# A one-core transformer layer with routed experts: activations turned by VectorE in 32x32 squares, expert weights loaded in consecutive rows

## The chip, the cores and the metric

The kernel runs on one core of one Trainium2 chip. The metric is device time in microseconds: 712.67 as the median of three runs (710.99 to 712.89). PE is TensorE (PEld its weight loads), DVE is VectorE, ACT is ScalarE, POOL is GpSimd, and SP is the queue that issues the large loads. All data are float32.

## The reference

One layer over 512 latent tokens and 256 context tokens, width 1024: modulated norm, one input projection, neighbourhood attention beside a bidirectional recurrence, an output projection with a gated residual, and then a mixture of 16 experts of which each token takes two. The part around the change is the last:

```python
def _moe(h, router_w, router_b, w1, w3, w2):
    aff = jax.nn.sigmoid(jnp.einsum('bld,de->ble', h, router_w))
    ...  # the best group of 4 experts, the top 2 experts in it, gates that add up to one
    for e in range(N_EXPERTS):
        y = (jax.nn.silu(h @ w1[e]) * (h @ w3[e])) @ w2[e]
        out = out + gates[..., e:e + 1] * y
```

w1 and w3 are 1024 x 512 for each expert, w2 is 512 x 1024; h is the normed latent stream, scaled and shifted by two rows computed from the condition vector. All weights of all experts are read once: 16 times 6.3 MB.

## The kernel before

**The expert loop.** The router sorts the (token, expert) pairs into tiles of 32 rows, each tile of one expert; in these data there are 44. PE keeps 32 rows as its loaded operand and lets 256 columns of weights pass, with four column groups of the array working on four quarters of the outputs. So a row of 1024 numbers lies as four quarters of 256 on four groups of 32 partitions, and a tile is a square of 128 partitions x 256.

For tile n the work is this. POOL fetches the rows by index from DRAM (`gather`, L478, buffer `xg`, two of them). ACT copies them (`next_rows`, L730, into `xrow`), PE turns the copy in two 128x128 pieces (`turn_rows`, L1606), DVE scales (L1238) and shifts (L1240) the result into `hsT`. PE multiplies by w1 and w3 (`products`, L1598: 8 slices of 128 inputs, 4 column groups). ACT takes the Silu of one half (L719) and DVE multiplies by the other (L1244) into `eact`. PE turns `eact` (`turn_act`, L1611), ACT copies it to `eT` (L723). PE multiplies by w2 (`rows_out`, L1621), DVE applies the gate (L1251), and POOL adds the rows by index into a DRAM array (`scatter`, L482). Before each fetch and each store by index, ACT copies a column of indices (L736, L742).

**The order around it.** It is written out by hand for each engine, and each engine goes strictly in its order. PE's is: products(n), turn_rows(n+1), rows_out(n-1), turn_act(n). ACT's is: Silu(n), copy of the turned activations(n), copy of the rows n+2, index for the fetch of n+4, index for the store of n-1. POOL's is the store of tile n-1, then the fetch of tile n+4. A buffer `xg` is fetched again once it was copied, so each fetch hangs on the copy of the tile two before it.

**The weights.** SP loads them in chunks of 2 MB, three to an expert: two of w1 and w3 together (L308, 128 partitions x 4 pieces of 2 KB for each matrix) and one of w2 (L311, 128 partitions x 4 pieces of 4 KB). There are 11 places for chunks (`homes`); chunk n takes the place of chunk n-11 after the last tile that used it (`sp.wait_ge(yt_ps if part == 2 else h_ps, after)`). The stores and fetches by index go over another queue of the same 16 DMA engines.

**Earlier users of the same layout.** The scale and shift rows `ab2` are summed over partitions by PE (`reduce_mod`, L1366, four times) and biased by DVE (`reduced`, L910). `router` (L1541) turns the normed tokens for the routing product, 32 turns in all.

## Time and profile before

| | us |
|---|---|
| median of 3 runs | 712.67 |
| lowest and highest | 710.99, 712.89 |
| the profiled execution | 713.67 |
| its span | 711.9 |
| expert loop, first product to the last `rows_out` | 423.36 to 697.15 |

The page gives 634.1 us (89%) of PE busy, 339.1 of DVE, 232.0 of ACT and 176.3 of POOL. Busy sums say little here: matmuls overlap, and each stage has another limit. The chain of waits tells which engine's work the end hung on; the windows tell how full the DMA engines were (their share can pass 1 because packets overlap) and how much they moved.

### The profile page before, as it was taken

What the parts mean: (1) busy time and instruction counts of PE and PEld (TensorE: products, weight loads), DVE (VectorE), ACT (ScalarE), POOL (GpSimd) and SP (SyncE); (2) the same over time, 40 slices, a digit from 0 to 9 for tenths busy, and PEclk for the clock granted to TensorE, in tenths of its full rate; (3) what the DMA queues carried; (4) which work ended last, traced back from release to release, by engine and by line L of the source; (5) the groups of instructions that cost most, each with busy time, mean ns of one, the idle gap of its engine ahead of it and who ended that gap; (6) DMA issues with size and microseconds to landing.
All of it is one profiled execution on the core that took longest, in us unless ns stands there. A gap on an engine that the chain in (4) does not pass through costs nothing.

```text
span 711.9 us, 15114 instructions
## 1 busy us (share of the span) xinstructions
PE 634.1 (89%) x5905; PEld 348.9 (49%) x5905; DVE 339.1 (48%) x794; ACT 232.0 (33%) x600; POOL 176.3 (25%) x201
## 2 busy tenths in 40 slices
PE   0799999899998997999999349999999999999991
PEld 0446544445444444555557325555555555555550
DVE  4513999456777957777662622222222222222220
ACT  5312201258887114555457101221122212222110
POOL 3033781000000001000003022344444444344431
PEclk9999999989999999999998559999999999999996
DMA  7999438711205359400048992999999999999924
GB/s 220 387 313 290 131 118 292 239 60 36 81 1 177 115 188 267 124 2 1 1 180 293 408 361 81 370 382 380 378 377 379 378 382 375 379 383 384 331 35 133
DMA packets 83508, 167.55 MB, mean 235 GB/s; under 512 B 4149, under 2 KB 26321, under 8 KB 83457
## 3 DMA queue, kind: packets, MB, share of 16 engines
q1 hardware_dynamic: 71856, 145.78, 56.6%
q0 software_dynamic: 11472, 21.00, 11.8%
q8 instruction: 38, 0.62, 0.4%
q14 instruction: 14, 0.11, 0.0%
q10 hardware_dynamic: 128, 0.04, 0.0%
HBM read 155.52 MB, written 12.60 MB: 236 GB/s over the span
## 4 chain that ended last, share of the span: by engine, by line
PE 66%; DVE 17%; issue 6%; DMA 4%; ACT 4%; SPq 1%; POOLq 0%; DVEq 0%
PE bank L1598 23%; PE bank L1621 12%; PE bank L1516 7%; PE bank L1408 7%; DMA ring<-in_w_mod_dram 4%; PE bank L1333 3%; DVE acct L880 3%; DVE gax L880 3%; PE bank L1606 2%; PE bank L1493 2%; PE bank L1479 2%; PE bank L1468 2%; DVE pre L898 2%; PE bank L1611 2%; PE bank L1297 1%
## 5 line engine op out<-in xcount | busy, mean ns | idle before, releaser
L1408 PE MATMUL bank<-ring,hx 128*128 128x512 f32 x256 | 115.0, 605 | 2.7 <-DVE mix L933 2.7
L482 POOL DMA_INDIRECT out_quarters<-pre,cur_s x44 | 69.6, 1582 | 146.9 <-ACT cur_s L742 124.4
L1244 DVE TENSOR_TENSOR pre<-pre,bank 128x128 f32<-128x128 f32 x44 | 12.7, 288 | 161.9 <-ACT pre L719 147.2
L1408 PEld LDWEIGHTS bank<-ring,hx 128*128 128x128 f32 x256 | 49.0, 194 | 60.2 <-issue 59.5
L1598 PE MATMUL bank<-pre 128*32 128x256 f32 x1248 | 75.0, 386 | 2.1 <-DVE pre L1240 1.4
L1598 PE MATMUL bank<-ring,pre 128*32 128x256 f32 x1152 | 67.6, 380 | 0.2
L1516 PE MATMUL bank<-ring,mix 128*128 128x512 f32 x128 | 61.8, 604 | 0.2 <-DVE mix L1038 0.2
L1598 PEld LDWEIGHTS bank<-pre 128*32 128x32 f32 x1248 | 41.7, 111 | 26.8 <-issue 3.0
L719 ACT ACTIVATE pre<-bank 128x128 f32<-128x128 f32 x44 | 12.2, 278 | 118.6 <-PE bank L1598 118.6
L1598 PEld LDWEIGHTS bank<-ring,pre 128*32 128x32 f32 x1152 | 37.7, 110 | 22.4 <-issue 1.4
L1333 PE MATMUL bank<-hx,ring 128*128 128x256 f32 (+1 forms) x128 | 43.7, 502 | 1.4 <-DVE hx L858 1.4
L723 ACT ACTIVATE pre<-bank 128x128 f32<-128x128 f32 x44 | 12.2, 278 | 96.5 <-PE bank L1611 96.5
L1621 PE MATMUL bank<-pre 128*32 128x256 f32 x704 | 42.5, 382 | 0.6 <-DVE pre L1251 0.6
L1251 DVE SCALAR_TENSOR_TENSOR pre<-bank,hx,pre 128x256 f32<-128x256 f32 x44 | 21.3, 484 | 43.9 <-PE bank L1621 43.9
L451 POOL DMA_DIRECT2D pre<-pre x1 | 0.6, 563 | 154.9 <-ACT pre L656 154.9
L1333 PEld LDWEIGHTS bank<-hx,ring 128*128 128x128 f32 x128 | 24.7, 195 | 20.2 <-issue 17.6
L1621 PE MATMUL bank<-ring,pre 128*32 128x256 f32 x544 | 32.9, 382 | 0.0
L461 POOL DMA_DIRECT2D xn_quarters<-pre x4 | 2.2, 545 | 115.9 <-DVE pre L1057 115.6
L880 DVE SCALAR_TENSOR_TENSOR acct<-ring,cs,acct 128x256 f32<-128x256 f32 x56 | 29.1, 520 | 2.0
L1516 PEld LDWEIGHTS bank<-ring,mix 128*128 128x128 f32 x128 | 22.0, 193 | 15.2 <-issue 14.8
L1621 PEld LDWEIGHTS bank<-pre 128*32 128x32 f32 x704 | 20.8, 109 | 15.5 <-issue 3.5
L1340 PE MATMUL bank<-hx,ring 128*128 128x512 f32 x64 | 27.6, 592 | 0.0
(282 smaller groups left out, 1019.5 us busy)
## 6 DMA issues: line engine op xcount, KB each, us to landing
pre<-in_exp_w_dram SPq DMA_DIRECT2D x28, 1024.0 KB
ring<-in_exp_w_dram SPq DMA_DIRECT2D x24, 1024.0 KB
ring<-in_w_mod_dram SPq DMA_DIRECT2D x16, 1024.0 KB, 5.1
pre<-in_exp_w_dram SPq DMA_DIRECT2D x8, 2048.0 KB
ring<-in_exp_w_dram SPq DMA_DIRECT2D x6, 2048.0 KB
ring<-in_w_in_dram SPq DMA_DIRECT2D x5, 2048.0 KB, 16.8
ring<-in_w_mod_dram SPq DMA_DIRECT2D x4, 2048.0 KB, 19.4
mix<-in_exp_w_dram SPq DMA_DIRECT2D x6, 1024.0 KB
```

Of the source, the lines that this page charges most:

```text
L482: g.indirect_dma_start(out=acc_dram, out_offset=bass.IndirectOffsetOnAxis(ap=cur_s[par][:].bitcast(U32), axis=0), in_=ysb[par], in_offset= ...
L880: ins = v.scalar_tensor_tensor(out=dst, in0=src[:, k, :], scalar=cs[:, k, 0:1], in1=dst, op0=ALU.mult, op1=ALU.add)
L898: ins = v.scalar_tensor_tensor(out=uc[:, m, 0:UO], in0=ur[:, k:k + UO], scalar=tap(k), in1=uc[:, m, 0:UO], op0=ALU.mult, op1=ALU.add)
L1251: v.scalar_tensor_tensor(out=ysb[par], in0=Y_[:, 0:QD], scalar=gate_tab[:, bass.ds(2 * h + par, 1)], in1=gfx4, op0=ALU.mult, op1=ALU.mult) ...
L1333: ins = te.matmul(B[bank][:, 0:n], slot[:, k, P * m:P * (m + 1)], hxT[:, k, lo:lo + n], start=(k == 0), stop=(k == KD - 1))
L1340: ins = te.matmul(B[4 + m % 2][:, :], slot[:, k, P * m:P * (m + 1)], hxT[:, k, 0:T], start=(k == 0), stop=(k == KD - 1))
L1408: ins = te.matmul(B[bank][:, :], hxT[:, k, P * j:P * (j + 1)], slot[:, k, :], start=(k == 0), stop=(k == KD - 1))
L1468: ins = te.matmul(B[SB[p % 2][z]][:, c0:c0 + 256], qT[o:o + HD, m, P * t:P * (t + 1)], kT[o:o + HD, m, k0:k1], start=True, stop=True)
L1479: ins = te.transpose(B[5][:, P * q:P * (q + 1)], prob[:, b, P * q:P * (q + 1)], ident[:])
L1516: ins = te.matmul(B[YB[hf]][:, :], mix[:, k, P * j:P * (j + 1)], out_at[hf][0][:, k, :], start=(k == MW), stop=(k == MW - 1))
L1598: ins = te.matmul(H_[R * q:R * (q + 1), 0:2 * P].rearrange("p (w n) -> p w n", w=2), hsT[:, at:at + R], w[:, k % 4, :, P * q:P * (q + 1)], ...
L1621: ins = te.matmul(Y_[R * q:R * (q + 1), 0:QD], eT[:, R * c:R * (c + 1)], w[:, c, QD * q:QD * (q + 1)], start=(c == 0), stop=(c == 3))
```

## The change

Four edits belong together. (1) PE turns nothing in the expert loop. DVE's 32x32 transpose takes the fetched rows straight from `xg` (`take_rows`), and turns the gated activations (in `gated`). It turns each 32x32 square by itself, so input number 8p+k of a row comes to partition p in slice k, instead of 128k+p. (2) The weights follow: partition p holds the consecutive rows 8p to 8p+7 of w1 and w3, and 4p to 4p+3 of w2. Each load is then one piece of 8 KB a partition (w1, w3) or 16 KB (w2). (3) The router, its weights, the scale and shift rows and their bias take the same numbering, for which PE loads every eighth column, and three small loads on POOL bring the bias and the gain in that order. (4) ACT loses both copies; DVE shifts the next tile's rows first, then gates, turns, applies the output gate, and takes the rows of the tile after next.

```diff
@@ -251,12 +251,12 @@
         def chunk13(e, part):
-            return homes[(3 * e + part) % NH].rearrange("p (k w n) -> p k w n", k=4, w=2)
+            return homes[(3 * e + part) % NH].rearrange("p (w k n) -> p k w n", k=4, w=2)
-        H_, X_, T_, Y_ = B[2], B[0], B[4], B[5]
+        H_, Y_ = B[2], B[5]
...
@@ -305,10 +305,12 @@
                     for w, src in enumerate((exp_w1, exp_w3)):
-                        sp.dma_start(chunk13(e, part)[:, :, w, :], src[0, ORDER[e], 512 * part:512 * (part + 1), :].rearrange(
-                            "(k p) n -> p k n", p=P)).then_inc(csem[n % NH], 16)
+                        sp.dma_start(chunk13(e, part)[:, :, w, :],
+                                     src[0, ORDER[e]].rearrange("(p k) n -> p k n", p=P)[
+                                         :, 4 * part:4 * part + 4, :]).then_inc(csem[n % NH], 16)
                 else:
-                    sp.dma_start(chunk2(e), exp_w2[0, ORDER[e]].rearrange("(k p) n -> p k n", p=P)).then_inc(csem[n % NH], 16)
+                    sp.dma_start(chunk2(e), exp_w2[0, ORDER[e]].rearrange("(p k) n -> p k n", p=P)).then_inc(
+                        csem[n % NH], 16)
...
@@ -399,7 +401,9 @@
                         l_q[0:H, 0:TR * TC]).then_inc(tab_in, 16)
-            g.dma_start(rw[:], router_w.rearrange("(k p) e -> p k e", p=P)).then_inc(rw_in, 16)
+            for z, src in enumerate((b_mod[0, 4 * D:5 * D], b_mod[0, 3 * D:4 * D], norm_ffn[0])):
+                g.dma_start(ffn_row[:, z, :], src.rearrange("(p k) -> p k", p=P)).then_inc(ffn_in, 16)
+            g.dma_start(rw[:], router_w.rearrange("(p k) e -> p k e", p=P)).then_inc(rw_in, 16)
             g.dma_start(rb[:],
...
@@ -490,7 +494,7 @@
             for n in (2, 3):
-                pool.wait_ge(xr_ready, n - 1)
+                pool.wait_ge(rows_taken, n - 1)
                 gather(slot_tok[:, n:n + 1], n % 2)
...
@@ -718,21 +721,10 @@
-            def turned(n):
-                act.wait_ge(t2_ps, n + 1)
-                a.activation(eT, T_[:, 0:P], ACT.Copy).then_inc(t2_ev, 1)
-            def next_rows(h, par):
-                act.wait_ge(xg_in[par], 16 * h + 16)
-                if not isinstance(h, int) or h + par:
-                    act.wait_ge(t_ps, 2 * h + par)
-                a.activation(xrow, xg[par], ACT.Copy).then_inc(xr_ready, 1)
-                act.wait_ge(xr_ready, 2 * h + par - 1)
+                act.wait_ge(rows_taken, 2 * h + par - 1)
...
@@ -743,44 +735,32 @@
-            next_rows(0, 0)
-            next_rows(0, 1)
-                if not isinstance(gt, int) or gt:
-                    act.wait_ge(yt_ps, gt)
-                turned(gt)
-            next_rows(1, 0)
-            next_rows(1, 1)
-            next_rows(2, 0)
-                next_rows(h + 1, 1)
-                next_rows(h + 2, 0)
-            next_rows(half + 1, 1)
-            next_rows(half + 2, 0)
...
@@ -905,9 +885,11 @@
                 dve.wait_ge(red_ps, n + 1)
-                dst = ab2[:, 1 - n // 2, 4 * (n % 2):4 * (n % 2 + 1)]
-                jc = C_BMOD + 3 * KD + 4 * n
-                v.tensor_tensor(dst, B[7][:, 0:4], col[:, jc:jc + 4], ALU.add).then_inc(red_ev, 1)
+                if n == 0:
+                    dve.wait_ge(ffn_in, 48)
+                m0, z = HD * (n % 2), 1 - n // 2
+                v.tensor_tensor(ab2[m0:m0 + HD, z, :], B[7][m0:m0 + HD, 0:KD], ffn_row[m0:m0 + HD, z, :],
+                                ALU.add).then_inc(red_ev, 1)
...
@@ -1226,22 +1208,39 @@
-            def wide(n):
-                return ab2[:, n, :].rearrange("p (c k) -> p k c", k=2).unsqueeze(3).to_broadcast([P, 2, CB, R])
-            def quads(ap):
-                return ap.rearrange("p (k c t) -> p k c t", k=2, c=CB)
-            def rows_ready(n):
-                dve.wait_ge(t_ps, n + 1)
-                v.tensor_tensor(quads(xm), quads(X_[:, 0:QD]), wide(0), ALU.mult).then_inc(xm_ready, 1)
-                dve.wait_ge(xm_ready, n + 1)
-                v.tensor_tensor(quads(hsT), quads(xm), wide(1), ALU.add).then_inc(hs_ready, 1)
+            def wide(z):
+                return ab2[:, z, :].unsqueeze(2).to_broadcast([P, KD, R])
+            def blocks(ap):
+                return ap.rearrange("p (b t) -> p b t", b=KD)
+            def take_rows(h, par):
+                n = 2 * h + par
+                dve.wait_ge(xg_in[par], 16 * h + 16)
+                if not isinstance(n, int) or n:
+                    dve.wait_ge(hs_ready, n)
+                v.transpose(blocks(xm), xg[par].rearrange("p (t b) -> p b t", b=KD)).then_inc(rows_taken, 1)
+                dve.wait_ge(rows_taken, n + 1)
+                v.tensor_tensor(blocks(xm), blocks(xm), wide(0), ALU.mult).then_inc(xm_scaled, 1)
+            def shift_rows(n):
+                if not isinstance(n, int) or n:
+                    dve.wait_ge(h_ps, n)
+                dve.wait_ge(xm_scaled, n + 1)
+                v.tensor_tensor(blocks(hsT), blocks(xm), wide(1), ALU.add).then_inc(hs_ready, 1)
+                if not isinstance(n, int) or n:
+                    dve.wait_ge(t2_ev, n)
+                if not isinstance(n, int) or n:
+                    dve.wait_ge(yt_ps, n)
+                dve.wait_ge(act_ready, n + 1)
+                v.transpose(eT.rearrange("p (b t) -> p b t", b=4), eact.rearrange("p (t b) -> p b t", b=4)).then_inc(t2_ev, 1)
...
@@ -1251,30 +1250,39 @@
-            dve.sem_inc(t2_ev, 1)
-            rows_ready(0)
+            take_rows(0, 0)
+            shift_rows(0)
+            take_rows(0, 1)
-                dve.wait_ge(t2_ps, gt)
+                shift_rows(gt + 1)
-                rows_ready(gt + 1)
-            gated(0)
-            rows_ready(1)
+            tile_step(0)
+            take_rows(1, 0)
+            take_rows(1, 1)
-            with dve.Fori(1, half + 1) as h:
+            take_rows(2, 0)
+            with dve.Fori(1, half) as h:
+                take_rows(h + 1, 1)
-            tile_step(2 * half + 3)
+                take_rows(h + 2, 0)
+            tile_step(2 * half + 1)
+            scaled(half, 0)
+            take_rows(half + 1, 1)
+            tile_step(2 * half + 2)
+            scaled(half, 1)
+            gated(2 * half + 3)
...
@@ -1362,8 +1370,10 @@
                     pe.wait_ge(red_ev, n)
-                for q in range(4):
-                    ins = te.matmul(B[7][:, q:q + 1], acct[:, P * q:P * (q + 1)], ones[:, 0:1], start=True, stop=True)
+                for k in range(KD):
+                    ins = te.matmul(B[7][HD * (n % 2):HD * (n % 2 + 1), k:k + 1],
+                                    acct[:, :].rearrange("p (m k) -> p m k", k=KD)[:, :, k], ones[:, 0:1], start=True,
+                                    stop=True)
                 ins.then_inc(red_ps, 1)
...
@@ -1539,7 +1549,7 @@
                     ins = te.transpose(B[RB[j % 2] + k // 4][:, P * (k % 4):P * (k % 4 + 1)],
-                                       xn[:, j, P * k:P * (k + 1)], ident[:])
+                                       xn[:, j, :].rearrange("p (m k) -> p m k", k=KD)[:, :, k], ident[:])
                     if k % 4 == 3:
...
@@ -1589,30 +1599,21 @@
                 pe.wait_ge(hs_ready, n + 1)
+                if not isinstance(n, int) or n:
+                    pe.wait_ge(act_ready, n)
                 for k in range(KD):
                     w = chunk13(e, k // 4)
-                    at = P * (k % 2) + R * (k // 2)
                     for q in range(CB):
                         ins = te.matmul(H_[R * q:R * (q + 1), 0:2 * P].rearrange("p (w n) -> p w n", w=2),
-                                        hsT[:, at:at + R], w[:, k % 4, :, P * q:P * (q + 1)], start=(k == 0),
+                                        hsT[:, R * k:R * (k + 1)], w[:, k % 4, :, P * q:P * (q + 1)], start=(k == 0),
                                         stop=(k == KD - 1))
-            def turn_rows(n):
-                pe.wait_ge(xr_ready, n + 1)
-                for z in range(2):
-                    ins = te.transpose(X_[:, P * z:P * (z + 1)], xrow[:, P * z:P * (z + 1)], ident[:])
-                ins.then_inc(t_ps, 1)
-            def turn_act(n):
-                pe.wait_ge(act_ready, n + 1)
-                te.transpose(T_[:, 0:P], eact, ident[:]).then_inc(t2_ps, 1)
             def rows_out(n1, e):
-                pe.wait_ge(t2_ev, n1 + 1)
+                pe.wait_ge(t2_ev, n1)
                 pe.wait_ge(y_ev, n1)
...
@@ -1622,24 +1623,18 @@
-            turn_rows(0)
             pe.wait_ge(plan_in, 1)
-            pe.wait_ge(t2_ev, 1)
             pe.wait_ge(gf_ev, 1)
                 tiles = pe.value_load(plan[0:1, e:e + 1], min_val=1, max_val=MAXT)
-                base = pe.value_load(plan[0:1, NE + ORDER[e]:NE + ORDER[e] + 1], min_val=0, max_val=MAXT) if e else 0
+                base = pe.value_load(plan[0:1, NE + ORDER[e]:NE + ORDER[e] + 1], min_val=2, max_val=MAXT) if e else 0
                 products(base, e, True)
-                turn_rows(base + 1)
                 if e:
                     rows_out(base, e - 1)
-                turn_act(base)
                 with pe.Fori(1, tiles) as t:
                     products(gt, e, False)
-                    turn_rows(gt + 1)
                     rows_out(gt, e)
-                    turn_act(gt)
             total = pe.value_load(plan[0:1, 3 * NE - 1:3 * NE], min_val=NE - 2, max_val=MAXT // 2 - 2) * 2 + 4
```

PE in the loop of the second expert, before: `products` is L1598, `rows_out` L1621, the turns are L1606 and L1611.

```order
L1637 ISA
L1598 MATMUL bank<-pre 32x256 x32
L1604 REGISTER_ALU
L1606 MATMUL bank<-ident,hx 128x128 x2
L1621 MATMUL bank<-ring,pre 32x256 x16
L1611 MATMUL bank<-ident,pre 128x128
```

The same place now (`products` is L1609, `rows_out` L1622):

```order
L1634 ISA
L1609 MATMUL bank<-pre 32x256 x32
L1622 MATMUL bank<-ring,pre 32x256 x16
L1634 REGISTER_ALU
L1634 COMPARE_AND_BRANCH
```

The three turns are gone, and the two products follow each other directly.

DVE in its loop, one tile, before: scale and shift of the next tile's rows are L1238 and L1240, the gating L1244, the output gate L1251.

```order
L1244 TENSOR_TENSOR pre<-pre,bank 128x128
L1237 REGISTER_ALU
L1238 TENSOR_TENSOR pre<-bank,ab 128x256
L1240 TENSOR_TENSOR pre<-pre,ab 128x256
L1249 REGISTER_ALU
L1251 ISA
L1251 SCALAR_TENSOR_TENSOR pre<-bank,hx,pre 128x256
```

The same tile now: shift L1232, gating L1239, its turn L1243, output gate L1250, turn of the fetched rows L1223, scale L1225.

```order
L1232 TENSOR_TENSOR pre<-pre,ab 128x256
L1238 REGISTER_ALU
L1239 TENSOR_TENSOR pre<-pre,bank 128x128
L1243 STREAM_TRANSPOSE pre<-pre 128x128
L1248 REGISTER_ALU
L1250 ISA
L1250 SCALAR_TENSOR_TENSOR pre<-bank,hx,pre 128x256
L1220 ISA
L1222 ISA
L1223 STREAM_TRANSPOSE pre<-hx 128x256
L1224 REGISTER_ALU
L1225 TENSOR_TENSOR pre<-pre,ab 128x256
```

DVE has two instructions more for each tile, and the one that frees the fetch buffer (L1223) now stands behind the output gate, which waits for `rows_out`.

## Rows read from the trace of the kernel before

**Rows 1.** The chain of waits of the whole span, shares by line.
```profile
PE bank L1598 23%; PE bank L1621 12%; PE bank L1516 7%; PE bank L1408 7%; DMA ring<-in_w_mod_dram 4%; PE bank L1333 3%; DVE acct L880 3%; DVE gax L880 3%; PE bank L1606 2%; PE bank L1493 2%; PE bank L1479 2%; PE bank L1468 2%; DVE pre L898 2%; PE bank L1611 2%; PE bank L1297 1%
```

**Rows 2.** The chain in order of time, one tile: start us, us, what.
```profile
497.67 3.59 PE bank L1598 x64
501.26 0.37 PE bank L1606 x2
501.63 1.86 PE bank L1621 x32
503.50 0.26 PE bank L1611
```

**Rows 3.** The chain: products of tiles 0, 1 and 43, and the end.
```profile
427.93 0.70 PE bank L1598 x12
...
430.10 3.66 PE bank L1598 x64
...
688.52 3.59 PE bank L1598 x64
...
692.48 1.91 PE bank L1621 x32
...
695.22 2.15 PE bank L1621 x32
```

**Rows 4.** Timeline: start us, us, engine line ..., [idle before <- releaser]; the loop's start.
```profile
415.69 1.06 POOL L478 DMA_INDIRECT pre<-xn_quarters,slot_tok  x1 [23.43 <-DVE slot_tok L1224]
421.23 0.42 ACT L730 ACTIVATE hx<-pre 128x256 f32<-128x256 f32 x1 [23.90 <-DMA pre<-xn_quarters,slot_tok]
423.36 3.49 PE L1598 MATMUL bank<-pre 128*32 128x256 f32 x32 [0.98 <-DVE pre L1240]
```

**Rows 5.** Timeline, ACT and POOL, from one copy of a buffer to the next.
```profile
504.03 0.41 ACT L730 ACTIVATE hx<-pre 128x256 f32<-128x256 f32 x1
...
505.78 1.58 POOL L482 DMA_INDIRECT out_quarters<-pre,cur_s  x1 [3.04 <-ACT cur_s L742]
507.66 1.00 POOL L478 DMA_INDIRECT pre<-xn_quarters,cur_g  x1 [0.30 <-issue]
...
516.45 0.41 ACT L730 ACTIVATE hx<-pre 128x256 f32<-128x256 f32 x1
```

**Rows 6.** DMA queues: packets, MB, share of 16 engines over the span.
```profile
q1 hardware_dynamic: 71856, 145.78, 56.6%
q0 software_dynamic: 11472, 21.00, 11.8%
q8 instruction: 38, 0.62, 0.4%
```

**Rows 7.** Windows: stretch, us, engines' busy us (x), PEclk, DMA share, GB/s.
```profile
396.00:400.00 4.00, 0.56 (x8) 0.00 (x0) 3.38 (x19) 1.31 (x2) 0.00 (x0) 0.50 1.04 416
480.00:500.00 20.00, 20.00 (x333) 11.12 (x329) 4.60 (x12) 4.03 (x18) 7.89 (x7) 1.00 1.07 375
675.00:680.00 5.00, 5.00 (x87) 2.65 (x79) 0.76 (x2) 0.99 (x5) 1.58 (x1) 1.00 0.23 64
```

**Rows 8.** DVE groups by form: count | busy us, mean ns of one | idle before.
```profile
L1251 DVE SCALAR_TENSOR_TENSOR pre<-bank,hx,pre 128x256 f32<-128x256 f32 x44 | 21.3, 484 | 43.9 <-PE bank L1621 43.9
L1240 DVE TENSOR_TENSOR pre<-pre,ab 128x256 f32<-128x256 f32 x45 | 19.1, 425 | 1.5
L1244 DVE TENSOR_TENSOR pre<-pre,bank 128x128 f32<-128x128 f32 x44 | 12.7, 288 | 161.9 <-ACT pre L719 147.2 <-issue 14.7
L1053 DVE TENSOR_TENSOR hx<-hx,pre 128x512 f32<-128x512 f32 x8 | 5.5, 692 | 0.3
L976 DVE SCALAR_TENSOR_TENSOR mix<-mix,pre 128x512 f32<-128x512 f32 x4 | 4.2, 1062 | 0.1
```

**Rows 9.** The chain at the first reduction and at the router's turns.
```profile
143.44 1.87 PE bank L1366 x8
...
373.32 1.97 PE bank L1541 x16
```

More of the change, by code:

```diff
@@ L127, in build @@
         row_sum = small[:, 32:34]
+        ffn_row = small[:, 36:60].rearrange("p (z k) -> p z k", z=3)
         hsum = sb("hsum", [P, 2, 2, H])
@@ L136, in build @@
         xg = [pre[:, 20480:20736], hx[:, 4608:4864]]
-        xrow = hx[:, 4864:5120]
         xm = pre[:, 20736:20992]
@@ L181, in build @@
             xr_in y_ps x2_ready sq2 rt2 xn2_ready h2_ps h2_ev lg_ps aff_ready dch ach pch gw_z gw_in
-            rank_m oh_ready oh_used rank_ps plan_in xn_out tok_ready t_ps sil_ready act_ready t2_ps
-            t2_ev fin_out misc_in rw_in h_ps xm_ready hs_ready yt_ps y_ev cur_g_ready cur_s_ready
-            acc_in gf_ps gf_ev lane_set sil_warm pad_ready xr_ready bank_z row_sum_ready scale_ready
-            hc_ready""".split()
+            rank_m oh_ready oh_used rank_ps plan_in xn_out tok_ready sil_ready t2_ev fin_out misc_in
+            rw_in h_ps hs_ready yt_ps y_ev cur_g_ready cur_s_ready acc_in gf_ps gf_ev lane_set
+            sil_warm pad_ready bank_z row_sum_ready scale_ready hc_ready rows_taken xm_scaled
+            act_ready ffn_in""".split()
         (pool_step, slots_turned, vz, tr_ev2, xn_out1, rows_in, ident_s, consts_ready, cols_ps,
@@ L192, in build @@
          lg_ps, aff_ready, dch, ach, pch, gw_z, gw_in, rank_m, oh_ready, oh_used, rank_ps, plan_in,
-         xn_out, tok_ready, t_ps, sil_ready, act_ready, t2_ps, t2_ev, fin_out, misc_in, rw_in, h_ps,
-         xm_ready, hs_ready, yt_ps, y_ev, cur_g_ready, cur_s_ready, acc_in, gf_ps, gf_ev, lane_set,
-         sil_warm, pad_ready, xr_ready, bank_z, row_sum_ready, scale_ready, hc_ready) = [sem(n) for n in names]
+         xn_out, tok_ready, sil_ready, t2_ev, fin_out, misc_in, rw_in, h_ps, hs_ready, yt_ps, y_ev,
+         cur_g_ready, cur_s_ready, acc_in, gf_ps, gf_ev, lane_set, sil_warm, pad_ready, bank_z,
+         row_sum_ready, scale_ready, hc_ready, rows_taken, xm_scaled, act_ready, ffn_in) = [sem(n) for n in names]
         xg_in = [sem(f"rows_in{par}") for par in range(2)]
@@ L522, in _ @@
                     store_rows(h, par)
-            fetch_rows(half + 2, 0)
             for n in range(4):
@@ L1004, in _ @@
             link(v.tensor_scalar(ab2[:, 0, :], ab2[:, 0, :], 1.0, None, ALU.add))
-            link(v.tensor_tensor(ab2[:, 0, :], ab2[:, 0, :], col[:, C_NFFN:C_NFFN + 8], ALU.mult))
+            link(v.tensor_tensor(ab2[:, 0, :], ab2[:, 0, :], ffn_row[:, 2, :], ALU.mult))
             def score(p, z):
```

## The prediction

> **What bounds the kernel now.** I read the chain of waits first: `products` (L1598) and `rows_out` (L1621) carry 35% of the span, the turns 4% [rows 1]. In order of time the chain never leaves PE in the expert loop: 3.59 us of products, 0.37 until `rows_out`, 1.86 of it, 0.26 until the next products [rows 2]. Tile 1's products start at 430.10 and tile 43's at 688.52, so 42 periods of 6.15 us [rows 3]. PE's order is the bound. Two things run close behind it. The DMA engines are full: 375 GB/s at a share of 1.07, and only after 675 us do they fall to 0.23 [rows 7]; the last weights are needed at 692.48 [rows 3], so they are some 16 us early. And there is the loop of the fetch buffers. ACT copies one at 504.03, POOL issues the store at 505.78 and the next fetch into it at 507.66 [rows 5]; a fetch took 415.69 to 421.23, 5.54 us, with the weights flowing [rows 4]. So the buffer is full at about 513.2, after 9.2 us, and is used at 516.45, after 12.4 us, which is two tiles: 3.2 us to spare.
>
> **PE's turns.** Both turns go: 0.37 + 0.26 = 0.63 us a tile, and PE's own period becomes 5.52. No row shows `products` and `rows_out` side by side without a turn; the floor may lie 0.2 lower, since a turn uses the whole array and waits for all four column groups. What stands behind the waits that remain: `products`(n+1) now waits for the shift and for the gating of tile n. Both start when products(n) end, beside `rows_out` (1.86 us): shift 0.43 (L1240), Silu and gating 0.29 each (L1244's 128 elements), done by 1.1 [rows 8]. They stay hidden. `rows_out` waits for activations one tile old.
>
> **DVE.** It gains two transposes a tile. The trace has none. Nearest row: 256 elements a lane take 425 ns (L1240), 128 take 288 (L1244). From below, the same; from above, L976 reads with a large stride and takes 1062 against 692 for a plain one of the same 512 elements (L1053) [rows 8], 1.53 times: 0.65 and 0.44 us. I take 0.45 and 0.3. DVE's sum is then 0.43 + 0.29 + 0.3 + 0.48 + 0.45 + 0.43 = 2.4 us of a period: no bound by itself. But it goes in order, and it now frees the fetch buffer behind the output gate, which waits for `rows_out`: if the fetch is late, DVE stands at the transpose, and the next shift, so PE, stands behind it.
>
> **The loop of the fetch buffers, with larger weight packets.** This is what I expect to be late next. A weight packet now takes 56.6% x 16 x 711.9 / 71,856 = 90 ns for 2.0 KB on average [rows 6]. At the same rate the 8 KB piece takes 0.36 and the 16 KB piece 0.72. A store by index has 128 rows, 8 for each of the 16 engines, and the fetch is queued behind it. If an engine takes one packet of each queue in turn, each of the 8 waits for one weight packet: today 8 x 0.09 (w1, w3) or 8 x 0.18 (w2), then 8 x 0.36 or 8 x 0.72. That adds 2.2 or 4.3 us to the 9.2, and the transpose 0.1: 11.5 us while w1 and w3 flow, 13.6 while w2 does. By bytes, 2 to 1, the mean is 12.2, so 6.1 us a tile, 5.75 with w1 and w3 alone. Bounds: 5.52 if large packets do not hold the other queue up (PE's floor), and 6.45 if the fetch's own rows wait too (two more packets each: 12.0 and 14.7). I take 5.9, the mean of 5.75 and 6.1.
>
> The Trainium skill speaks against this term. Its page "DMA: Bandwidth & Descriptors", section "Queues, rings and completion order", says that an engine switches queues at packets only, and that a packet usually holds 9 to 17 descriptors. By that rule a store's eight rows would pass in one go and the term would vanish; by mine it decides. No row here shows the turns taken between queues.
>
> **Weights.** Larger pieces may move faster: 416 GB/s at a share of 1.04 where 4 KB rows are among the traffic, 375 at 1.07 in the loop [rows 7]. Bounds 0 and 11% (416/375); I take 5%, so the 236 us from 440 to 676 shrink by 12. The refill also starts 1.4 us earlier (below). The last weights then land near 662, and are needed at 692.48 less what PE gains. With the gain below, 680: hidden.
>
> **Before and at the edges.** Start: 421.23 to the first products at 423.36 is 2.13 us [rows 4]; transpose, scale and shift in a row are 0.45 + 0.43 + 0.43 + 0.1 = 1.4: -0.7. Tile 0's products end at 428.63 and tile 1's start at 430.10 [rows 3], 1.47 apart; Silu, shift and gating need 0.8: -0.7. End: between the last two `rows_out` 0.83 us pass (692.48 + 1.91 to 695.22) [rows 3]; now transpose 0.3, gate 0.48 and hand-overs: +0.1. The router's turns load every eighth column: eight turns take 1.97 us [rows 9], and some 20 of 32 are on the chain, 4.9 us. Bounds 0 and +2.6 (the 1.53 of above); I take +1. The first reduction takes 1.87 us for four products [rows 9] and has eight of half the width now: between -0.5 and +1.9, I take +0.5; the other three lie beside DVE's recurrences. POOL's three loads of small pieces stand where the router's weights are loaded, two stages before their use: nothing.
>
> On strides, "SBUF — State Buffer", section "Door 1: The DMA port swizzle (why `[64,N]` ≈ `[32,N]`)", of the Trainium skill says that float32 reads at steps over four elements change the 16-byte line each time and pay. The trace agrees in kind, with 1.53 times for L976. Both new patterns on PE and the row transposes step by eight.
>
> **The sum.** While weights flow (tile 1 to about tile 40, 662 us): 39 x (6.15 - 5.9) = 9.8. The last three periods at 5.52: 1.9. Edges 1.4 - 0.1. Before the loop: +1.5. Together -11.5. The profiled execution took 713.67, so 702.2; the median of the runs is 1.0 below it: 701. This case's own range is 692 to 707 (period 5.7 to 6.05). Chance 0.42.
>
> **Rivals.**
> - A, PE's floor holds and nothing else is late: 42 x 0.63 + 1.3 - 1.5 = 26.3: 686. For it: 3.2 us to spare in the buffer loop, and weights at 662 against a need at 666. It wants both the packet gain and no hold-up in the other queue. If PE's floor is lower, down to 680. Chance 0.27.
> - C, no hold-up but also no packet gain: the last weights land at 676 - 1.4 = 674.6, and 4.9 us of work follow (692.48 to 697.37), where the old end was 697.37: -17.9 + 1.5, so 696. Against it: the 416 GB/s. Chance 0.08.
> - D, slower: 16 KB packets are slow. The instruction queue's packets of 16 KB take 0.4% x 16 x 711.9 / 38 = 1.2 us each [rows 6]. A w2 load would be 8 x 1.2 = 9.6 us in place of 32 x 0.18 = 5.8; 37 loads are refills, 12.3 of them w2: +47 us, of which 16 are spare. With 1.5 before the loop that is 713 + 29 + 1 = 743. It decides from 0.88 us a packet on (0.72 + 16 / 12.3 / 8). Against it: these come singly, from another queue. Chance 0.05.
> - E, the buffer loop at its upper bound, above PE's old period: 6.45 gives 39 x 0.3 - 1.9 + 0.2 = +10: 722; at 6.2 it is about 712. Its place is DVE's wait at the row transpose; it decides from 12.3 us a loop on. Chance 0.18.
>
> **How the numbers follow.** No change means within 0.3%, 710.5 to 714.8, about what a measurement of this kernel can tell. Faster: B (the forecast) 0.42, A 0.27, C 0.08 and a third of E 0.06, so 0.83. Same: 0.04 of E. Slower: the rest of E and D, 0.13. The range 682 to 714 takes in B, C, nearly all of A and half of E; it leaves out about 0.17.
>
> **What would show it.** Right: PE with idle time ahead of `products`, put down to the shift (DVE) or its buffer, DVE idle ahead of the row transpose with the fetch as releaser, periods near 5.9 while weights flow and near 5.5 after them, and longer periods while w2 loads. A: periods near 5.5 throughout and no such wait. C: PE waits at an expert's first products or first `rows_out` while DMA is full to the end. D: DMA rate under 375 GB/s. A transpose over 0.65 us, or router turns over 3 us for eight, would make steps of the sum wrong.

## The result, and the profile after

The change made the kernel slower: 723.1 us (median of four runs, 723.0 to 726.2) against 711.8, a ratio of 1.0165 with a 95% interval of 1.0137 to 1.0194. The forecast was 701, range 682 to 714. In this section and below, kernels go by short names; `after` is the changed kernel. Times are medians over a kernel's fast runs; one run of w2small and one of order2, over 1.5% above the fastest of their kernel, are left out.

The page of after, with the chain of waits by line:
```profile
DMA pre<-xn_quarters,cur_g 14%; PE bank L1418 10%; PE bank L1526 7%; DMA hx<-xn_quarters,cur_g 7%; PE bank L1609 6%; PE bank L1341 6%; PE bank L1348 4%; DMA out_quarters<-hx 3%; PE bank L1622 3%; DMA ring<-in_w_mod_dram 2%; PE bank L1489 2%; PE bank L1503 2%; PE bank L1478 2%; DVE pre L1223 2%; POOL out_quarters L486 1%
```
Before, `products` and `rows_out` on PE carried 35% of the span [rows 1]. In after the two (L1609, L1622) carry 9%, and the fetches by index (`pre` and `hx` from `xn_quarters`) carry 21%. The bound of the loop has moved from TensorE to the queue of the indexed transfers.

The waits of after between 430 and 700 us (engine and line <- releaser: us in total, times, longest):
```profile
DVE pre L1250 <- DMA out_quarters<-pre,cur_s: 76.7, 28, 6.5
POOL out_quarters L486 <- ACT cur_s L734: 54.7, 14, 6.9
...
PEld bank L1609 <- DVE pre L1232: 26.6, 19, 2.9
...
PE bank L1622 <- issue: 17.6, 12, 4.1
DVE pre L1223 <- DMA hx<-xn_quarters,cur_g: 14.6, 16, 2.6
DVE pre L1223 <- DMA pre<-xn_quarters,cur_g: 12.4, 15, 1.7
```
The largest wait of VectorE is the output gate (L1250) waiting for an earlier *store* to land, so that its buffer is free: 76.7 us. The waits at the row transpose (L1223) for a *fetch*, which I had named as the place, are 27.0 us. On PE the same time shows as idle ahead of `products`, put down to the shift, and ahead of `rows_out`.

The timeline of after, ACT, POOL and DVE around one store buffer (start us, us; [idle before <- releaser]):
```profile
509.68 0.49 DVE L1250 SCALAR_TENSOR_TENSOR pre<-bank,hx,pre 128x256 f32<-128x256 f32 x1 [2.68 <-DMA out_quarters<-pre,cur_s]
...
510.74 0.65 DVE L1223 STREAM_TRANSPOSE pre<-pre 128x256 f32<-128x256 f32 x1 [0.58 <-DMA pre<-xn_quarters,cur_g]
...
511.51 0.20 ACT L728 ACTIVATE cur_g<-slot_tok 128x1 int32 x1 [5.77 <-DVE pre L1223]
511.62 0.20 ACT L734 ACTIVATE cur_s<-slot_tok 128x1 int32 x1
...
512.74 1.58 POOL L486 DMA_INDIRECT out_quarters<-pre,cur_s  x1 [3.21 <-ACT cur_s L734]
...
518.45 0.48 DVE L1250 SCALAR_TENSOR_TENSOR pre<-bank,hx,pre 128x256 f32<-128x256 f32 x1 [5.21 <-DMA out_quarters<-pre,cur_s]
519.03 1.93 PE L1622 MATMUL bank<-ring,pre 128*32 128x256 f32 x32 [2.52 <-issue]
...
522.89 0.48 DVE L1250 SCALAR_TENSOR_TENSOR pre<-bank,hx,pre 128x256 f32<-128x256 f32 x1 [0.94 <-DMA out_quarters<-pre,cur_s]
```
This is the loop that decides. The gate fills a buffer at 509.68, its store is issued at 512.74, and the gate that uses the buffer again, two tiles on, starts at 522.89: 13.2 us for two tiles, 6.6 each. Of it 3.06 lie between gate and store. In them the sums are ready, but the store's index is not: ScalarE copies it (L734) in order behind the fetch's index (L728), which waits for the row transpose (L1223), which waits for the *next* fetch. So this store stood behind a fetch, and with two buffers the gate two tiles on stood behind this store. It is no single case: between 430 and 700 us 31 transposes waited for a fetch and 28 gates for a store (the counts in the rows above). Over the 33 tiles gated between 440 and 660 us, gate to store is 3.4 us on average and the whole loop 13.4 us; in before it is 2.1 and 12.3.

The chain of after near the end, where the weights have all landed:
```profile
666.84 3.66 PE bank L1609 x64
670.50 1.73 PE bank L1622 x32
672.23 3.45 PE bank L1609 x64
675.68 1.73 PE bank L1622 x32
677.41 3.45 PE bank L1609 x64
680.87 1.73 PE bank L1622 x32
682.59 0.24 issue
682.83 3.66 PE bank L1609 x64
```
There `products` and `rows_out` follow each other with nothing between them: 5.18 us a tile inside an expert (672.23 to 677.41), about 5.6 where an expert changes, 5.36 over the run's mix. Before that the products that start at 457.98 and at 666.84 are 31 periods apart, 6.74 each:
```profile
457.98 1.94 PE L1609 MATMUL bank<-ring,pre 128*32 128x256 f32 x32
...
698.80 1.51 PE L1609 MATMUL bank<-ring,pre 128*32 128x256 f32 x24
```
Tile 1's products start at 431.14 and tile 43's at 698.80, 267.7 us, against 258.4 before [rows 3]: that is +9.2 of the +9.5 between the two spans (711.9 and 721.4).

The waits had a second cost. Twice in this loop TensorE had stood for over 3 us, and its granted clock fell to the lower of its two levels, 1.2 GHz in place of 2.4. The first of the two, on PE:
```profile
484.17 3.64 PE L1622 MATMUL bank<-pre 128*32 128x256 f32 x32 [3.24 <-issue]
487.55 4.79 PE L1609 MATMUL bank<-ring,pre 128*32 128x256 f32 x64
492.16 1.91 PE L1622 MATMUL bank<-pre 128*32 128x256 f32 x32
```
After 3.24 us of idle, `rows_out` takes 3.64 us where it takes 1.91 one tile later, and the products 4.79 in place of 3.66. By the clock records of the trace the lower level holds for 10.2 us of after's loop (483.1 to 489.9 and 636.7 to 640.1) and for nothing of before's. TensorE is busy for 8.9 of the 10.2 us, and that work would take half the time at the upper level, so the clock accounts for at most 4.5 us of the +9.2 (an estimate).

DMA in after, by windows (as [rows 7]), the queues (as [rows 6]), and from issue to landing, 440 to 660 us and from 672 us on:
```profile
480.00:500.00 20.00, 16.17 (x244) 9.03 (x234) 6.56 (x15) 1.43 (x8) 5.54 (x5) 0.83 1.03 399
...
675.00:680.00 5.00, 5.00 (x99) 3.62 (x92) 2.39 (x6) 0.59 (x3) 2.58 (x2) 1.00 0.35 54
```
```profile
q1 hardware_dynamic: 41136, 145.78, 53.3%
q0 software_dynamic: 11520, 20.88, 12.0%
```
```profile
out_quarters<-pre,cur_s POOLq DMA_INDIRECT x34, 9.9
hx<-xn_quarters,cur_g POOLq DMA_INDIRECT x17, 9.5
```
```profile
out_quarters<-pre,cur_s POOLq DMA_INDIRECT x8, 3.8
```
The larger pieces did move more: 399 GB/s where it was 375 (the 0.83 ahead of the share is the mean granted clock of that stretch). A store takes 9.9 us while they flow and 3.8 when they don't.

The new and changed instructions of VectorE (as [rows 8]), and the turns on PE's chain (as [rows 9]):
```profile
L1232 DVE TENSOR_TENSOR pre<-pre,ab 128x256 f32<-128x256 f32 x44 | 18.7, 425 | 33.5 <-PE bank L1609 32.4
L1243 DVE STREAM_TRANSPOSE pre<-pre 128x128 f32<-128x128 f32 x44 | 18.4, 418 | 26.5 <-PE bank L1622 24.7
L1223 DVE STREAM_TRANSPOSE pre<-hx 128x256 f32<-128x256 f32 x22 | 14.3, 648 | 14.7 <-DMA hx<-xn_quarters,cur_g 14.6
```
```profile
142.41 2.01 PE bank L1374 x16
...
375.50 2.02 PE bank L1551 x16
```

### The profile page after: what moved, and what is told of

Read it like the earlier page. It is cut to its first block, busy times and chain, and to the rows that moved or that the text cites. A ratio compares the mean times of both kernels' runs of the same rounds, so it can differ in the third digit from the quotient of the medians.

```text
span 721.4 us, 14927 instructions
## 1 busy us (share of the span) xinstructions
PE 610.0 (85%) x5803; PEld 359.9 (50%) x5803; DVE 384.1 (53%) x880; ACT 204.1 (28%) x511; POOL 177.1 (25%) x203
## 4 chain that ended last, share of the span: by engine, by line
PE 47%; DMA 27%; DVE 9%; issue 8%; ACT 4%; POOL 2%; SPq 1%; POOLq 1%; DVEq 0%; ACTq 0%
DMA pre<-xn_quarters,cur_g 14%; PE bank L1418 10%; PE bank L1526 7%; DMA hx<-xn_quarters,cur_g 7%; PE bank L1609 6%; PE bank L1341 6%; PE bank L1348 4%; DMA out_quarters<-hx 3%; PE bank L1622 3%; DMA ring<-in_w_mod_dram 2%; PE bank L1489 2%; PE bank L1503 2%; PE bank L1478 2%; DVE pre L1223 2%; POOL out_quarters L486 1%
## 5 line engine op out<-in xcount | busy, mean ns | idle before, releaser
L1418 PE MATMUL bank<-ring,hx 128*128 128x512 f32 x256 | 117.7, 616 | 2.7 <-DVE mix L915 2.7
L1609 PE MATMUL bank<-pre 128*32 128x256 f32 x1248 | 75.3, 386 | 19.9 <-DVE pre L1232 11.3
L1609 PE MATMUL bank<-ring,pre 128*32 128x256 f32 x1152 | 68.9, 385 | 6.8 <-DVE pre L1239 5.8
L1609 PEld LDWEIGHTS bank<-pre 128*32 128x32 f32 x1248 | 46.9, 111 | 44.4 <-DVE pre L1232 23.1
L728 ACT ACTIVATE cur_g<-slot_tok 128x1 int32 (+1 forms) x41 | 8.3, 203 | 210.0 <-DVE pre L1223 210.0
L1250 DVE SCALAR_TENSOR_TENSOR pre<-bank,hx,pre 128x256 f32<-128x256 f32 x44 | 20.7, 470 | 78.9 <-DMA out_quarters<-pre,cur_s 76.7
L1609 PEld LDWEIGHTS bank<-ring,pre 128*32 128x32 f32 x1152 | 43.5, 112 | 29.7 <-DVE pre L1232 9.2
L1622 PE MATMUL bank<-pre 128*32 128x256 f32 x704 | 44.3, 391 | 4.9 <-issue 4.0
L1622 PE MATMUL bank<-ring,pre 128*32 128x256 f32 x544 | 34.4, 394 | 12.7 <-issue 12.7
L1232 DVE TENSOR_TENSOR pre<-pre,ab 128x256 f32<-128x256 f32 x44 | 18.7, 425 | 33.5 <-PE bank L1609 32.4
L1622 PEld LDWEIGHTS bank<-pre 128*32 128x32 f32 x704 | 26.8, 112 | 18.6 <-issue 8.2
L1622 PEld LDWEIGHTS bank<-ring,pre 128*32 128x32 f32 x544 | 20.7, 113 | 24.1 <-issue 17.1
L1243 DVE STREAM_TRANSPOSE pre<-pre 128x128 f32<-128x128 f32 x44 | 18.4, 418 | 26.5 <-PE bank L1622 24.7
L722 ACT ACTIVATE pre<-bank 128x128 f32<-128x128 f32 x44 | 12.2, 278 | 70.8 <-PE bank L1609 68.8
## 6 DMA issues: line engine op xcount, KB each, us to landing
ring<-in_exp_w_dram SPq DMA_DIRECT2D x6, 2048.0 KB, 12.3
```

Of the source, the lines that this page charges most:

```text
L1232: v.tensor_tensor(blocks(hsT), blocks(xm), wide(1), ALU.add).then_inc(hs_ready, 1)
L1243: v.transpose(eT.rearrange("p (b t) -> p b t", b=4), eact.rearrange("p (t b) -> p b t", b=4)).then_inc(t2_ev, 1)
L1250: v.scalar_tensor_tensor(out=ysb[par], in0=Y_[:, 0:QD], scalar=gate_tab[:, bass.ds(2 * h + par, 1)], in1=gfx4, op0=ALU.mult, op1=ALU.mult) ...
L1418: ins = te.matmul(B[bank][:, :], hxT[:, k, P * j:P * (j + 1)], slot[:, k, :], start=(k == 0), stop=(k == KD - 1))
L1609: ins = te.matmul(H_[R * q:R * (q + 1), 0:2 * P].rearrange("p (w n) -> p w n", w=2), hsT[:, R * k:R * (k + 1)], w[:, k % 4, :, P * q:P * ( ...
L1622: ins = te.matmul(Y_[R * q:R * (q + 1), 0:QD], eT[:, R * c:R * (c + 1)], w[:, c, QD * q:QD * (q + 1)], start=(c == 0), stop=(c == 3))
```

## The experiments

Theory H: the large weight packets hold up the indexed rows on the other queue. Theory O: the order on VectorE (rows are taken behind the gate) is the cause, whatever the packets. Later theory L joined them: a loop of the store buffers through the in-order queues of three engines, which the packets stretch past TensorE's period. The ratio is to before, run beside it, with its 95% interval. "From first products" is the profiled span less the start of tile 0's products, which takes out the stages ahead of the loop; it is of one execution each.

| kernel | weight pieces w1, w3 / w2 | order | us | ratio | from first products |
|---|---|---|---|---|---|
| before | 2 / 4 KB | PE turns | 711.8 | 1 | 288.5 |
| beforebig | 8 / 16 | PE turns | 724.9 | 1.020 (1.015 to 1.026) | 300.2 |
| after | 8 / 16 | as changed | 723.1 | 1.0165 (1.014 to 1.019) | 296.5 |
| small | 2 / 4 | as changed | 705.5 | 0.990 (0.987 to 0.993) | 277.2 |
| w2small | 8 / 4 | as changed | 706.6 | 0.993 (0.990 to 0.996) | 280.4 |
| w13small | 2 / 16 | as changed | 704.3 | 0.989 (0.986 to 0.992) | 279.6 |
| mid | 4 / 4 | as changed | 697.9 | 0.981 (0.978 to 0.984) | 272.3 |
| order | 8 / 16 | rows taken ahead of gate | 730.9 | 1.027 (1.024 to 1.031) | 300.7 |
| order2 | 8 / 16 | and fetch ahead of store | 706.5 | 0.989 (0.983 to 0.996) | 276.6 |
| midorder2 | 4 / 4 | as order2 | 703.8 | 0.987 (0.985 to 0.990) | 276.4 |
| actswap | 8 / 16 | store's index first | 702.7 | 0.988 (0.985 to 0.992) | 273.5 |
| midact | 4 / 4 | store's index first | 698.3 | 0.982 (0.979 to 0.985) | 271.4 |
| w2smallact | 8 / 4 | store's index first | 697.7 | 0.981 (0.977 to 0.985) | 268.6 |
| floor | 4 / 4, w2 refills cut | store's index first | 683.2 | 0.956 (0.950 to 0.961) | 258.5 |

### The size of the pieces: small, w2small, w13small, mid

The row numbering stays consecutive; only the layout in SBUF changes, so that a partition's rows no longer lie side by side and are moved in smaller pieces. small makes both of these edits, w2small the second, w13small the first.
```diff
-  chunk13: rearrange("p (w k n) -> p k w n", k=4, w=2)
+  chunk13: rearrange("p (k w n) -> p k w n", k=4, w=2)       # 2 KB
-  chunk2:  rearrange("p (k n) -> p k n", k=4)                  # one load
+  chunk2:  rearrange("p (a b n) -> p a b n", a=2, b=2)         # two loads, b = 0, 1, 4 KB
```
mid has the second one, and for w1 and w3 pairs of rows:
```diff
+  chunk13: rearrange("p (a w b n) -> p a w b n", a=2, b=2, w=2)  # 4 KB
```

small:

> The kernel after with w1 and w3 stored in SBUF as before (pieces of 2 KB) and w2 in two loads of pieces of 4 KB; the numbering of the rows and VectorE's turns stay. Theory H (large weight packets hold up the rows fetched and stored by index on the other queue): the landing of a store falls from 9.9 to about 6 us, VectorE no longer waits for it (under 10 us in total, 73 now), the periods while weights flow are 5.2 to 5.6, and the time is 692 to 700, bound by the weights at 375 GB/s. Theory O (VectorE's own order is the cause: the fetch buffer is freed only behind the output gate, which waits for rows_out): piece size does not matter, periods stay at 6.3 on average, 715 to 723.

w2small:

> The kernel after with w2 alone in pieces of 4 KB (two loads); w1 and w3 stay at 8 KB. H, with one weight packet let past per packet of the index queue (10 packets per tile and engine, 0.31 us each at 8 KB, 0.63 at 16 KB): the long periods of 7 to 11 us, which go with w2's share of the traffic, go; 694 to 702. O: 715 to 723.

w13small:

> The kernel after with w1 and w3 in pieces of 2 KB; w2 stays at 16 KB. H: the long periods while w2 flows stay, and most of the loss with them: 706 to 718. O: 715 to 723.

mid:

> The kernel after with all expert weights in pieces of 4 KB (w1 and w3 two rows a piece, w2 in two loads of one row a piece). The three runs so far ended at 704 to 707, one with periods of 5.35 us until the weights ran out (2 KB and 4 KB, 377 GB/s in all), two with fuller rates and some long periods. Theory H with the weights as the second bound: at 4 KB the rate is near 390 GB/s and the hold-up half of that at 8 KB, so few periods over 6: 696 to 702. If only the rate counted it would be as small, 704 to 706; if hold-up were all, 688 to 694.

Measured: all four are 16 to 25 us faster than after, so O alone falls: VectorE's order is the same in all. In small the gate hardly waits for a store any more (its line L1252, 440 to 660 us):
```profile
DVE pre L1252 <- DMA out_quarters<-pre,cur_s: 3.1, 4, 1.3
```
But H missed the times of three of the four: small was expected at 692 to 700 and took 705.5, w2small at 694 to 702 and took 706.6, w13small at 706 or more and took 704.3. H was right on the mechanism and took too little account of a second bound, which it had named for small alone and too cheaply: once the loop is free, the arrival of the weights ends it. Windows of 480 to 580 us, in the order before, small, mid, after:
```profile
480.00:580.00 100.00, 99.50 (x1624) 55.17 (x1620) 24.51 (x64) 19.77 (x83) 41.81 (x33) 1.00 1.06 379
```
```profile
480.00:580.00 100.00, 97.91 (x1799) 66.61 (x1792) 46.41 (x114) 11.60 (x56) 47.87 (x38) 1.00 1.07 376
```
```profile
480.00:580.00 100.00, 97.33 (x1766) 67.31 (x1760) 48.04 (x109) 10.49 (x54) 46.55 (x37) 1.00 1.05 385
```
```profile
480.00:580.00 100.00, 80.43 (x1372) 50.93 (x1366) 37.38 (x85) 8.22 (x42) 36.50 (x29) 0.97 1.04 399
```
The last number is the rate: 379, 376, 385, 399 GB/s. The second is PE's busy time: before it is full of turns and products, in small and mid nearly full of products, in after it stands for a fifth of the time. small has the slack but the old rate, after the rate but no slack, mid enough of both, and is the fastest of the four, 697.9, inside its expectation.

The turns that an engine takes between its queues can be counted in the packet records of the traces. A store is 128 rows of 1 KB, 8 for each of 16 engines. From its first packet to its last (means over stores whose packets come in one unbroken burst, those at 16 KB over eight stores only):

| weight packets flowing beside it | one weight packet | store's burst | 1.3 + 8 packets |
|---|---|---|---|
| none | | 1.3 us | |
| 2 KB (small) | 0.084 us | 2.05 | 2.0 |
| 4 KB (mid) | 0.159 | 2.6 | 2.6 |
| 8 KB (after) | 0.309 | 3.5 | 3.8 |
| 16 KB (after) | 0.625 | 5.3 | 6.3 |

One weight packet or a little more goes by for each row of a store: per row 1.0 start during the burst at 8 and 16 KB, 1.25 at 4 KB, 1.6 at 2 KB. The last column, an estimate from one for each of an engine's eight rows, fits up to 8 KB and is 1.0 us too high at 16. The size of the pieces adds to the burst only: from issue to the first packet a store takes 4.8 us in before, small and after alike, and 2.1 where no weights flow. From issue to the last packet (medians) that makes 7.0 us for a store in before, 6.9 in small, 9.4 in after; for the fetch queued behind it 5.8, 5.8 and 8.7.

### Large pieces in the kernel before: beforebig

```diff
   (before.py, turns on TensorE kept; loads and layout as in after)
-  src[0, ORDER[e], 512 * part:512 * (part + 1), :].rearrange("(k p) n -> p k n", p=P)
+  src[0, ORDER[e]].rearrange("(p k) n -> p k n", p=P)[:, 4 * part:4 * part + 4, :]
-  exp_w2[0, ORDER[e]].rearrange("(k p) n -> p k n", p=P)
+  exp_w2[0, ORDER[e]].rearrange("(p k) n -> p k n", p=P)
```

> The kernel before, TensorE's turns and all, with the weight loads of after (pieces of 8 and 16 KB); what is computed with them is no longer the reference's, since each partition holds other rows of the weights than the turned tokens. H: the loop of the fetch buffers, 9.2 us of 12.4 before, gets 3.8 us longer on average and more while w2 flows, so it goes over TensorE's 12.3: 714 to 730, with PE idle at the rows' copy. O: the turns on TensorE keep the loop short and the faster weights are not needed: 709 to 714.

Measured 724.9, as H says; O's 709 to 714 is out. Its waits, 440 to 660 us:
```profile
DVE pre L1252 <- DMA out_quarters<-pre,cur_s: 53.3, 20, 4.4
ACT hx L731 <- DMA hx<-xn_quarters,cur_g: 29.6, 14, 4.4
ACT hx L731 <- DMA pre<-xn_quarters,cur_g: 27.9, 15, 3.8
```
None of these waits on DMA was among those of before in that stretch, and its granted clock stays at the upper level throughout the loop, so here the packets cost time without the clock's part. The pieces alone cost 13.1 us with the turns on TensorE (711.8 to 724.9) and 17.6 with the turns on VectorE (705.5 to 723.1). Moving the turns is worth 6.3 us at the old sizes, where the weights then end the loop, and 1.8 at the new ones, which is within the spread of the runs (721.2 to 726.7 and 723.0 to 726.2).

### The order: order, order2, midorder2

```diff
                 tile_step(2 * h + 1)
-                scaled(h, 0)
                 take_rows(h + 1, 1)
+                scaled(h, 0)
```

and for order2 and midorder2, on GpSimd:
```diff
                 for par in range(2):
-                    fetch_rows(h + 2, par)
+                    fetch_rows(h + 2 + par, 1 - par)
                     store_rows(h, par)
```

order:

> The kernel after, large pieces kept; on VectorE take_rows goes ahead of the output gate (scaled), so that the fetch buffer is freed without waiting for a store's landing. O (the order on VectorE is the cause): the chain of two tiles loses the store's wait of 2 to 3 us, 700 to 710. H: the index queue's rows wait for weight packets as before and the loop of the store buffers takes over: 716 to 724.

order2:

> order, and on GpSimd each fetch is issued ahead of the store that it came after, so that its rows aren't queued behind that store's. O: 696 to 706. H: some of it, since only eight rows fewer stand ahead of a fetch, 710 to 720.

midorder2:

> mid and order2 together, the version that the experiments point to. Both theories: the index loops have slack, TensorE runs at periods of 5.35 while the weights are there, and the weights' rate is the bound: 692 to 700.

Both theories missed order: 730.9, slower than after by 8. The timeline shows a tile of it:
```profile
504.99 0.64 DVE L1223 STREAM_TRANSPOSE pre<-pre 128x256 f32<-128x256 f32 x1 [5.85 <-DMA pre<-xn_quarters,cur_g]
...
506.00 0.48 DVE L1250 SCALAR_TENSOR_TENSOR pre<-bank,hx,pre 128x256 f32<-128x256 f32 x1
...
506.58 3.64 PE L1622 MATMUL bank<-pre 128*32 128x256 f32 x32 [4.74 <-issue]
...
507.32 1.58 POOL L486 DMA_INDIRECT out_quarters<-pre,cur_s  x1 [7.07 <-DVE pre L1250]
...
509.20 1.00 POOL L482 DMA_INDIRECT pre<-xn_quarters,cur_g  x1 [0.30 <-issue]
```
VectorE stood 5.85 us for a fetch; the gate stood behind it, the store behind the gate, and on GpSimd the next fetch behind the store, so each fetch of the loop starts late. This tile also stands at the lower clock: its `rows_out` takes 3.64 us, not 1.9. The lower level holds for 23.9 us of order's loop (10.2 of after's), with 21.5 us of TensorE work in it, so up to 10.8 us of order's time are the clock's, and up to 6.3 of the 8 between it and after (an estimate as above). Nearly all by which it missed H's 716 to 724 can be the clock, then; O's 700 to 710 it misses without it. order2 breaks the last of these links, and with the same packets it takes 24.4 us less (706.5, between the two expectations); the lower clock doesn't occur in its loop. midorder2 missed its 692 to 700: it is 5.9 us slower than mid; of its span's 7.5 over mid's, 3.3 lie ahead of tile 0, and I did not follow the rest.

### The order on ScalarE: actswap, midact, w2smallact

```diff
                 activation(2 * h + 1)
-                gather_index(h + 2, 1)
                 scatter_index(h, 0)
+                gather_index(h + 2, 1)
```
(the same in the other half of the loop and ahead of it; nothing else)

actswap:

> The kernel after, large pieces kept; on ScalarE each index copy for a store goes ahead of the index copy for the fetch. In after a store's index waits on ScalarE behind the fetch's, which waits for VectorE's transpose, which waits for the next fetch: from 509.68 (gate) to 512.74 (store issued) 3.06 us, where some 1 would do. Theory L (a loop of the store buffers through this chain: landing 9.9 to 11.8 us, 3 us of hand-overs, 2 buffers, 6.6 us a tile; the large packets and the order are needed together): about 2 us a loop, 1 us a tile go, 33 tiles: 690 to 704. H alone (the packets, whatever the order): 716 to 724.

midact:

> mid with the same exchange of index copies on ScalarE. mid is at TensorE's period until its weights run out, so L and H both expect little: 694 to 699, the weights' rate of 385 GB/s being the bound; VectorE's wait for stores, 40 us in mid, falls under 10.

w2smallact:

> w2small (w1 and w3 at 8 KB, w2 at 4 KB) with the same exchange. L: the store's loop gets the slack that it lacks there (71 us of waits), the rate is 392 GB/s in place of 385: 691 to 698, level with midact or just ahead. H alone: as w2small, 704 to 709.

Measured: actswap 702.7, with the packets of after, 20.4 us less than after. Its timeline, to be held against the one of after above:
```profile
501.43 0.48 DVE L1250 SCALAR_TENSOR_TENSOR pre<-bank,hx,pre 128x256 f32<-128x256 f32 x1 [2.88 <-DMA out_quarters<-pre,cur_s]
...
512.49 0.48 DVE L1250 SCALAR_TENSOR_TENSOR pre<-bank,hx,pre 128x256 f32<-128x256 f32 x1 [1.98 <-DMA out_quarters<-pre,cur_s]
...
513.81 1.58 POOL L486 DMA_INDIRECT out_quarters<-pre,cur_s  x1 [3.59 <-DVE pre L1250]
```
Gate to store is 1.32 us (512.49 to 513.81) in place of 3.06, and the loop is 11.1 us (501.43 to 512.49) in place of 13.2, close to TensorE's 10.7 for two tiles. Over the 37 tiles gated between 440 and 660 us, the means are 1.5 (3.4 in after) for gate to store and 11.9 (13.4) for the loop. Of the 20.4 us at most 4.5 are the clock's, which stays at the upper level in actswap's loop. The store still takes as long:
```profile
out_quarters<-pre,cur_s POOLq DMA_INDIRECT x37, 10.2
```
H alone is out, as O alone is: it takes the packets *and* the chain. The loop is freed, but not quite: VectorE still waits 59.8 us for stores here. midact and w2smallact are level with mid, as expected; w2smallact has the shortest loop, 268.6 us from tile 0's products. mid, midact and w2smallact beat both kernels, by 2% the one before.

### What bounds the best ones: floor

```diff
+  lanes = P if n < NH else 16          # refills of w2: 16 of 128 partitions
-  sp.dma_start(chunk2(e)[:, :, b, :], ...
+  sp.dma_start(chunk2(e)[0:lanes, :, b, :], ...
```

> midact with the refills of w2 cut to 16 of 128 partitions (13 of the 37 refills; what is computed with them is not the reference's). Theory W (mid and midact are bound by the weights' arrival: midact runs at 5.18 to 5.7 us a tile until tile 30, then waits for weights, the last of which land at 666.6): TensorE's own period holds to the end, 42 periods of 5.36 us: 676 to 684. If something else ended the loop (VectorE, the index queue): 692 to 699.

Measured 683.2, within the expectation. In midact the chain near the end reads:
```profile
644.43 22.18 DMA ring<-in_exp_w_dram
...
677.25 0.41 DVE pre L1245
```
Its last weights land at 666.6, and the last `rows_out` ends at 680.1. So mid and midact are bound by the arrival of the weights, and some 15 us below them lies TensorE's own period. floor also takes traffic off the index queue's engines (340 GB/s in place of 384 over 480 to 580 us), but that was not what held midact: between 440 and 660 us its VectorE waits 0.2 us for a fetch and never for a store, and its TensorE is 98% busy from 480 to 580.

## Why the prediction was wrong

**TensorE.** Right: both turns left the chain, and the floor is 5.36 a tile; I had 5.52, "0.2 lower" allowed. That a turn waits for all four column groups, the reason given for it, no run tests.

**VectorE's transposes.** They take 648 and 418 ns, my upper bounds (0.65 and 0.44); I had taken 0.45 and 0.3. That the bounds fit so well is in part luck: their 1.53 compares two different operations (L976 and L1053), not a read with and without a stride. It adds 0.3 us to a period with slack, and little to the loop.

**The packets.** Right in kind, and nearly in size. I added 2.2 us (8 KB) and 4.3 (16 KB), by bytes 2.9; a fetch now takes 8.7 us to its last packet, 5.8 before: 2.9. The page "DMA: Bandwidth & Descriptors" of the Trainium skill, which I had let speak against it ("Queues, rings and completion order": a turn passes a whole packet, usually of 9 to 17 descriptors), would have made the term vanish. The bursts of 1.3, 2.05, 2.6, 3.5 and 5.3 us decide against it: here an engine let about one weight packet go by for each single row of a store. Turns by packets fit the traces, if each of these rows is a packet of its own; 9 to 17 rows in one turn don't.

**The loop: the step that failed.** "So the buffer is full at about 513.2, after 9.2 us, ... 3.2 us to spare" counted the *fetch* buffers alone. I priced the store's burst only as what stands ahead of a fetch, never as the store's own landing. Two buffers hold the sums too; a gate waits until the store of two tiles ago has landed. That loop is 3.06 us from gate to store and 10.2 on to the next gate, 13.2 (3.4, 10.0 and 13.4 as means), where TensorE wants 10.7 and my fetch loop said 11.5 to 13.6 with a mean of 11.8. In before, all 43.9 us of the gate's waits ended with PE [rows 8], none with a store, so its loop was hidden: 2.1 us from gate to store and 7.0 to the store's last packet, 9.1 of 12.3. I had not looked for it because it did not wait. Through ScalarE's and GpSimd's order each loop also passes through the other. actswap shows the term: with the packets unchanged, 1.7 us fewer between gate and store (1.9 as means) give back 20.4 us.

**The mean.** I took 5.9, a mean over 5.75 and 6.1. But 6.1 was already the mean over all weights, and 5.75 holds for w1 and w3 alone; halving between them had no reason, and 6.1 in the same sum gives 709. The 31 periods from 457.98 on were 6.74 on average and uneven: by the packet records, the 13 in which w2 has over 0.4 of the weights' bytes are 7.8 us on average, the 18 others 6.0. A long wait is not paid back by a short loop, since no period falls under 5.18: the mean of a maximum is over the maximum of the means. This too pushed 5.9 up.

**The clock.** The prediction has no term for it. The waits that it did not foresee let the granted clock fall for 10.2 us of the loop, which adds at most 4.5 us.

**Weights.** Rate right: 399 against 379 GB/s over 480 to 580, 5.3%; I had 5. But "hidden" was wrong for the fast case: with the loop free, the weights end it (midact 698.3), close to rival C's 696, though C reckoned 4.9 us of work behind the last weights, and there are 13.5. Rival A's 686 was within reach only of floor, where a third of the refills is cut. Without the failed step this change gives what actswap gives, 702.7, near the forecast of 701 and inside its 692 to 707; with 4 KB pieces as well it is 698. Neither is 686.

**Before the loop.** The router's turns take 2.02 us (1.97 before) and the first reduction 2.01 (1.87): +0.1 each, where I took +1 and +0.5; strides of eight cost next to nothing on PE here, whatever the page "SBUF — State Buffer" of the Trainium skill ("Door 1") says of float32 reads at such steps. The first products start at 424.94, 1.6 us later than before, but among the fourteen kernels profiled they start anywhere from 419.2 to 428.1 with nearly the same instructions ahead. These starts go with the time at the lower clock ahead of them, by the clock records: 51.2 us where they start at 419.2 (beforebig), 54.6 in before, 58.0 in after, 64.9 where they start at 427.8 and 428.1 (order, order2). So the 1.6 may be the clock's and need not be the edits'.

**The rivals.** E came true in sign and nearly in time (712 to 722; decided "from 12.3 us a loop on"), but its place was the gate's wait for a store, 76.7 us, more than the transpose's wait for a fetch, 27.0; and I gave it 0.18, because I had counted one loop of two. D is out: 399 GB/s, 0.63 us for a 16 KB weight packet where 1.2 was read from another queue. Its sum was also loose: 47 less 16 is 31, not 29.

## What to carry to other kernels

Before a change makes packets larger on one queue, list *every* loop of buffers that the other queue serves, the stores too, hidden or not, and price each with its hand-overs against the new period. A wait that the profile doesn't show today has a slack that can be read only from the timeline: from the filling of a buffer to its next use. Where two loops pass through the same in-order engines, a wait put in one is paid in both; issue what is ready (here the store's index) ahead of what must wait. And try the middle size: with after's order 4 KB pieces were the fastest of the four settings with smaller pieces (697.9), and with the store's index first 4 KB throughout and 8 KB with 4 KB were level (698.3 and 697.7).
